# Differential attention: the four value projections move into the head loop, one ahead of every second head's value product

## The reference

```python
def diff_mixer(h, w_in, qk_norm_g, lam_vecs, subln_g, w_out, rel_table, lam_init):
    q, k, v = jnp.split(h @ w_in, [DIFF_QK, 2 * DIFF_QK], axis=-1)
    q = rms_norm(q.reshape(B, S, 8, 2, 64), qk_norm_g[0]) * (64 ** -0.5)
    k = rms_norm(k.reshape(B, S, 8, 2, 64), qk_norm_g[1])
    ...
    p1 = softmax(q1 @ k1.T + bias); p2 = softmax(q2 @ k2.T + bias)
    out = (p1 - lam * p2) @ v                       # per head, v is 256 x 128
    out = rms_norm(out, subln_g) * (1.0 - lam_init)
    return out.reshape(B, S, DIFF_V) @ w_out
```

## Time and profile before

| what | value |
|---|---|
| median of 3 runs | 1779.64 us (1777.1 to 1780.9) |
| the profiled execution | 1776.03 us, of which the span from first to last instruction is 1774.2 us |
| PE busy | 89% of the span |
| DVE, ACT, POOL busy | 52%, 41%, 8% |
| mean granted TensorE clock | 0.918 of full speed |
| the diff stage | about 887 to 1070 us of the span |

### The profile page before, as it was taken

One profiled execution on the slowest core, in us unless ns is written; L12 is line 12 of the kernel. 1 busy time (PEld: TensorE's weight loads), 2 busy tenths in 40 slices (PEclk: granted clock), 3 DMA queues, 4 the chain that ended last, 5 costly groups with the idle time before them and its releaser, 6 DMA issues.

```text
span 1774.2 us, 23807 instructions
## 1 busy us (share of the span) xinstructions
PE 1583.0 (89%) x10412; PEld 1437.9 (81%) x10412; DVE 916.0 (52%) x1006; ACT 728.0 (41%) x780; POOL 148.2 (8%) x147
## 2 busy tenths in 40 slices
PE   5999998588799999999998669999799987789997
PEld 4999997587689998999998459999777773679996
DVE  4666655667354445544545645444642246354443
ACT  4544543566244434443444434444432233244332
POOL 2000001055000000000023001000130000010000
PEclk9999997899899999999999779999886775789999
DMA  7788861412145554655584016555330011035551
GB/s 249 243 278 262 271 215 49 141 50 94 56 159 190 184 179 136 213 184 180 184 208 151 24 41 212 190 189 183 92 119 24 24 48 48 24 110 194 180 183 70
DMA packets 197777, 258.75 MB, mean 146 GB/s; under 512 B 4781, under 2 KB 178122, under 8 KB 197546
## 3 DMA queue, kind: packets, MB, share of 16 engines
q1 hardware_dynamic: 194672, 248.59, 42.9%
q0 software_dynamic: 2752, 8.57, 1.7%
q10 hardware_dynamic: 250, 0.08, 0.0%
HBM read 255.91 MB, written 1.31 MB: 145 GB/s over the span
## 4 chain that ended last, share of the span: by engine, by line
PE 75%; DVE 10%; POOL 5%; ACT 4%; issue 4%; DMA 1%; SPq 0%; DVEq 0%; POOLq 0%; ACTq 0%
PE bank L175 15%; PE bank L176 15%; PE bank L177 15%; PE acc L175 7%; PE acc L176 7%; PE acc L177 7%; DVE w_lo L155 3%; ACT w_hi L149 2%; PE bank L1752 2%; PE acc L1726 1%; POOL rstd L759 1%; POOL arena L734 1%; POOL arena L735 1%; PE acc L1794 1%; POOL rstd L310 1%
## 5 line engine op out<-in xcount | busy, mean ns | idle before, releaser
L155 DVE TENSOR_TENSOR w_lo<-w_raw,w_hi 128x2048 fp32r<-128x2048 f32 x236 | 548.7, 2326 | 498.3 <-ACT w_hi L149 498.3
L149 ACT ACTIVATE w_hi<-w_raw 128x2048 fp32r<-128x2048 f32 x236 | 448.8, 1908 | 385.6 <-PE bank L177 290.7
L175 PE MATMUL bank<-h_hi,w_hi 128*128 128x256 f32 (+1 forms) x1872 | 540.5, 289 | 8.2 <-DVE h_lo L266 5.1
L176 PE MATMUL bank<-h_lo,w_hi 128*128 128x256 f32 (+1 forms) x1872 | 538.9, 288 | 0.0
L177 PE MATMUL bank<-h_hi,w_lo 128*128 128x256 f32 (+1 forms) x1872 | 538.7, 288 | 0.0
L175 PEld LDWEIGHTS bank<-h_hi,w_hi 128*128 128x128 f32 x1872 | 363.6, 194 | 16.0 <-issue 12.8
L176 PEld LDWEIGHTS bank<-h_lo,w_hi 128*128 128x128 f32 x1872 | 363.4, 194 | 3.2
L177 PEld LDWEIGHTS bank<-h_hi,w_lo 128*128 128x128 f32 x1872 | 363.2, 194 | 1.9
L175 PE MATMUL acc<-w_hi,act_hi 128*128 128x512 f32 x416 | 164.0, 394 | 0.8 <-issue 0.8
L176 PE MATMUL acc<-w_lo,act_hi 128*128 128x512 f32 x416 | 163.4, 393 | 0.0
L177 PE MATMUL acc<-w_hi,act_lo 128*128 128x512 f32 x416 | 162.7, 391 | 0.0
(11 more groups left out here) (267 smaller groups left out, 1675.6 us busy)
## 6 DMA issues: line engine op xcount, KB each, us to landing
w_raw<-in_ffn_w_gu SPq DMA_DIRECT2D x88, 1024.0 KB, 5.1
w_raw<-in_ffn_w_down SPq DMA_DIRECT2D x44, 1024.0 KB, 4.9
w_raw<-in_w_ada SPq DMA_DIRECT2D x24, 1024.0 KB, 5.9
w_raw<-in_w_ffn_in SPq DMA_DIRECT2D x22, 1024.0 KB, 5.1
w_raw<-in_gla_w_in SPq DMA_DIRECT2D x12, 1024.0 KB, 5.4
w_raw<-in_diff_w_in SPq DMA_DIRECT2D x12, 1024.0 KB, 5.2
w_raw<-in_w_ffn_out SPq DMA_DIRECT2D x11, 1024.0 KB, 4.9
w_raw<-in_w_in SPq DMA_DIRECT2D x9, 1024.0 KB, 5.2
```

The source lines that it names most:

```text
L149: eng.activation(w_hi[:, slot, :], w_raw[:, slot, :], ACT.Copy).then_inc(sem("unit_hi"), 1)
L155: eng.tensor_tensor(w_lo[:, slot, :], w_raw[:, slot, :], w_hi[:, slot, :].bitcast(F32), ALU.subtract).then_inc(sem("unit_split"), 1)
L175: pe.matmul(out_, a[0], b[0], start=first, stop=False)
L176: pe.matmul(out_, a[0], b[1], start=False, stop=False)
```

## The change

Only the units 8 to 11 (v) move. PE and ACT do units 0 to 7 ahead of the attention, and ACT's squares follow unit 7's copy. In the head loop, heads 0, 2, 4 and 6 each get one unit, 8 + h/2: on PE between the scores of h+2 and the value product of h, into bank 3, with a wait for ACT's copy of it before the value product; on ACT after the copy of the transposed probabilities (`split_hi` of unit 11 + h/2 and the copy out of bank 3); on DVE the `split_lo` of unit 11 + h/2 between `combine(h)` and `output(h-1)`. The value products of even and odd heads now use the two halves of bank 2, and PE waits for one more output copy (`output(h-1)` in place of `output(h-2)`).

```diff
@@ -910,17 +910,16 @@
 
                 split_hi(eng, u + j + 3)
                 eng.wait_ge(sem("unit_used"), u + j + 1)
-                eng.activation(diff_qkv[:, j, :, :].rearrange("p t c -> p (t c)"), bank[j % 3][:, :], ACT.Copy)\
+                b = bank[j % 3] if j < 8 else bank[3]
+                eng.activation(diff_qkv[:, j, :, :].rearrange("p t c -> p (t c)"), b[:, :], ACT.Copy)\
                     .then_inc(sem("diff_copied"), 1)
 
-            for j in range(9):
+            for j in range(8):
                 unit(j)
             for t in range(2):
                 eng.wait_ge(sem("diff_copied"), 4 * t + 4)
                 c = slice(t * 4 * TT * UC, (t + 1) * 4 * TT * UC)
                 eng.activation(diff_sq[:, c], flat_qkv()[:, c], ACT.Square).then_inc(sem("diff_squared"), 1)
-            for j in range(9, N_DIFF_IN):
-                unit(j)
             eng.wait_ge(sem("diff_dots"), 2)
             eng.activation(diff_dot[:, :], diff_dot[:, :], ACT.Exp).then_inc(sem("diff_exp_dots"), 1)
             for hp in range(4):
@@ -945,6 +944,8 @@
                 if h >= 2:
                     eng.wait_ge(sem("diff_pv"), h - 1)
                 eng.activation(diff_pt[:, h % 2, :], bank[h % 2][:, :], ACT.Copy).then_inc(sem("diff_pt_ready"), 1)
+                if h % 2 == 0:
+                    unit(8 + h // 2)
             eng.wait_ge(sem("diff_o_copied"), DH)
             for t in range(TT):
                 eng.activation(diff_osq[:, t * D:(t + 1) * D], diff_o[:, t, :], ACT.Square)\
@@ -977,12 +978,10 @@
                 eng.tensor_reduce(ssq[:, t * n_group:(t + 1) * n_group],
                                   diff_sq[:, c].rearrange("p (g d) -> p g d", d=DDH), AX.X, ALU.add)\
                     .then_inc(sem("diff_sums"), 1)
-                split_lo(eng, u + 12 + t)
             eng.wait_ge(sem("mixer_rstd"), mixer_index(name, 1))
             g = flat_qkv()[:, 0:4 * TT * UC].rearrange("p (g d) -> p g d", d=DDH)
             eng.tensor_tensor(g, g, rstd[:, 0:n_group].unsqueeze(2).broadcast_to([P, n_group, DDH]), ALU.mult)\
                 .then_inc(sem("diff_scaled_q"), 1)
-            split_lo(eng, u + 14)
             eng.wait_ge(sem("diff_exp_dots"), 1)
             eng.scalar_tensor_tensor(diff_neg_lam[:, :], diff_dot[:, 1:2], LAM_INIT, diff_dot[:, 0:1], ALU.subtract,
                                      ALU.subtract).then_inc(sem("diff_lam"), 1)
@@ -1031,7 +1030,7 @@
             def output(h):
                 eng.wait_ge(sem("diff_pv"), h + 1)
                 eng.tensor_copy(diff_o[:, :, h * P:(h + 1) * P],
-                                bank[2 + h % 2][:, 0:TT * P].rearrange("p (t c) -> p t c", t=TT))\
+                                bank[2][:, (h % 2) * S:(h % 2 + 1) * S].rearrange("p (t c) -> p t c", t=TT))\
                     .then_inc(sem("diff_o_copied"), 1)
 
             logits(0)
@@ -1039,6 +1038,8 @@
                 if h + 1 < DH:
                     logits(h + 1)
                 combine(h)
+                if h % 2 == 0:
+                    split_lo(eng, u + 11 + h // 2)
                 if h >= 1:
                     output(h - 1)
             output(DH - 1)
@@ -1089,11 +1090,11 @@
             h0 = h_ready_before(name)
 
             def unit(j, h_wait=None):
-                b = bank[j % 3]
+                b = bank[j % 3] if j < 8 else bank[3]
                 natural_columns(pe, u + j, [b[:, 0:UC], b[:, UC:2 * UC]], S, h_wait)\
                     .then_inc(sem("unit_used"), 1)
 
-            for j in range(N_DIFF_IN):
+            for j in range(8):
                 if j >= 3:
                     pe.wait_ge(sem("diff_copied"), j - 2)
                 unit(j, None if j else h0)
@@ -1104,7 +1105,7 @@
                     pe.wait_ge(sem("diff_scaled_q"), 1)
                 if n == 4:
                     pe.wait_ge(sem("diff_scaled_k"), 1)
-                    pe.wait_ge(sem("diff_copied"), N_DIFF_IN)
+                    pe.wait_ge(sem("diff_copied"), 8)
                 b = acc_bank[n] if n < 4 else bank[n - 4]
                 for hh in range(2):
                     for t in range(TT):
@@ -1138,12 +1139,19 @@
                 last.then_inc(sem("diff_p_transposed"), 1)
                 if h + 2 < DH:
                     scores(h + 2)
+                if h % 2 == 0:
+                    if h >= 2:
+                        pe.wait_ge(sem("diff_copied"), 8 + h // 2)
+                    else:
+                        pe.wait_ge(sem("diff_k_ready"), 4)
+                    unit(8 + h // 2)
+                    pe.wait_ge(sem("diff_copied"), 9 + h // 2)
                 pe.wait_ge(sem("diff_pt_ready"), h + 1)
-                if h >= 2:
-                    pe.wait_ge(sem("diff_o_copied"), h - 1)
+                if h >= 1:
+                    pe.wait_ge(sem("diff_o_copied"), h)
                 for t in range(TT):
                     for k in range(TT):
-                        last = pe.matmul(bank[2 + h % 2][:, t * P:(t + 1) * P],
+                        last = pe.matmul(bank[2][:, (h % 2) * S + t * P:(h % 2) * S + (t + 1) * P],
                                          diff_pt[:, h % 2, k * S + t * P:k * S + (t + 1) * P],
                                          diff_qkv[:, 8 + h // 2, k, (h % 2) * P:(h % 2 + 1) * P],
                                          start=k == 0, stop=k == 1)
```

## The result

The median went from 1780.3 us (the kernel before, timed beside it) to 1816.1 us; the ratio is 1.0194 with an interval of 1.0162 to 1.0226. The forecast was 1811, range 1800 to 1819.

The account below looks back on a forecast made before the run. PE matmuls bound most of the kernel, but a chain off PE bounds the stretch ahead of the loop and a PE-DVE circle the loop. Loop +42.8 (41.4 plus clock 1.4), ahead -10.7: +32, forecast 1811 us, range 1800 to 1819.

Parts of the forecast that it names:

- VectorE's waits for `w_hi`: Sign in the head loop: DVE's largest wait would be on ACT's split, some 6 to 8 us each.
- Part 1: Ahead of the head loop: earlier squares and sums start POOL 9.3 us earlier, a removed split gives 1.4; 10.7 us gained.
- PE's idle time: Sign ahead of the loop: PE waits 22 us from 941, with scores of head 0 at about 970.3.
- The removal of VectorE's split: Ahead of the loop: without DVE's split queued before them, copies of k follow the transposes and scores start 1.4 us earlier.
- Part 2: Head loop: unit, ACT's split and DVE's split lie end to end, 10.5 us in heads 0, 2, 4, 9.9 in 6; together 41.4.
- the circle: Head loop's repeating dependency: transposes and scores on PE (3.17 or 1.77 us), then logits and combine on DVE (3.47 us).
- The clock, +1.4: Head loop: heads 1, 3, 5 run low (+3.2 us), heads 2 and 4 high behind a 5 us burst (-1.8).
- D: Rival, head loop: low clock in even heads too, units partly at half speed; +4 to +8 us, 1817; chance 11%.
- A: Rival, head loop: dense units keep the clock high through the gaps; -8.2 us, 1803, still slower; chance 12%.
- B: Rival, head loop: DVE runs ahead, logits(h+2) not behind the unit; even head 11.3 us, total +12.5, 1792; chance 3%.
- C: Rival, head loop: units hide in PE's idle time during DVE's work; loop 55.6 us, total +1.2, 1781; chance 4%.

Follow-up runs that it names:

- e7: Kernel before with only the change's banks: value products in two halves of bank 2, PE waiting for output(h-1); 1782.6 us, ratio 1.0006.
- e5: Kernel before, all units still ahead of the attention, with only ACT's squares moved behind unit 7 and VectorE's sums ahead of its splits; 1775.0 us, ratio 0.9962.
- e1: Changed kernel with VectorE's split of the next unit behind combine of the odd head instead of the even one; 1793.5 us, ratio 1.006.
- e3: Changed kernel with ScalarE, in the loop, copying the unit's product before splitting the next unit; 1818.5 us, ratio 1.0205.
- e10: Changed kernel with unread identity products in PE's gaps: 18 behind each unit, 16 behind the first scores, 6 behind each value product; 1802.2 us, ratio 1.0115.
- e2: Changed kernel with ScalarE copying before splitting and VectorE's split behind combine of the next even head, the last behind head 7; 1783.5 us, ratio 1.0012.
- e6: Kernel before with early squares and back-to-back sums, and VectorE's split of unit 14 moved behind the copies of k; 1772.6 us, ratio 0.995.
- e9: Kernel before with unread identity products on PE: 16 behind the scores of heads 0 and 1, 6 behind each value product; 1771.0 us, ratio 0.9934.
- e4b: Changed kernel with 18 unread identity products on PE behind each of the four units; 1807.6 us, ratio 1.0138.
- e4: Changed kernel with 64 unread identity products on PE behind each of the four units; 1838.4 us, ratio 1.0327.

## Why the prediction was right, point by point

The forecast was +32 us; the two lengths say +35.5 and the medians +35.9. One of the signs named in the forecast was mis-sized: VectorE's waits for `w_hi` are 11.0 us each in the mean and not 6 to 8, because they begin where VectorE ends its combine, and take in TensorE's transposes and scores as well. It has no part in the sum. The loop ended at 1067.3, not 1064.

- **Part 1, 10.7 us earlier.** 10.3 measured at the scores of head 0, counted from ACT's `w_hi` of unit 7; the 11.3 of the table has 1.0 more, which is the high clock of those scores (2.00 us, not 3.50), and luck, as e7 shows. The sums were done at 948.94 (944.46 + 4.48), 8.7 us behind ACT's `w_hi` of unit 7 and not 18.1 as before; the scores of head 0 started at 969.83 (forecast 970.3, and the earlier end of unit 7 alone moves them by 0.9). PE's idle time of 22.28 us was forecast as 22. The removal of VectorE's split: the copies of k began 1.1 us behind the start of their transposes, where 0.6 was forecast. The lock of the shared port, which the Trainium skill's page "SBUF — State Buffer" ("SBUF: two separate sides") describes, shows again in the changed kernel and in e5: a small operation of VectorE, queued in the place of the split, took from 962.19 to 965.77, the end of GpSimd's scaling (960.02 + 5.73 = 965.75). Timeline of VectorE; the same operation took 0.15 us in the kernel before:

```profile
962.19 3.58 DVE L986 SCALAR_TENSOR_TENSOR arena<-arena 128x1 f32<-128x1 f32 x1
```

- **Part 2, the unit and both splits on the circle.** Right in kind (chain, waits, e1 against e3) and in size: with the clock held up (e10) head 2 takes 15.74 us. Measured in the changed kernel: 16.96, 17.31, 17.29 and 14.55 for heads 0, 2, 4 and 6.
- **The clock, +1.4.** This is the term that was mis-sized: about +5.4 in place of +1.4 (46.8 - 41.4). Odd heads were right (6.68). Heads 2 and 4 were forecast at the high clock, 15.74, and took 1.6 more each; head 6 took 14.55 and not 13.4. The step that failed is the sentence that heads 2 and 4 come behind a 5 us burst and so run high, as head 1 did: they ran high for the transposes only (0.66 and 0.69), then low for the scores and the beginning of the unit. Each unit ran partly at the low clock: 6.46, 6.66, 6.61 and 7.23 us from its start to ACT's `w_hi` at granted clocks of 0.93, 0.90, 0.91 and 0.79, against a pitch of 5.76. For heads 0 to 5 e10 shows that nothing but the clock was missing. Why the clock fell after 0.66 us of transposes in one place and not in another is left open.
- **Rivals.** D (low clock everywhere, 1817) came half true, and 1816.1 lies nearer to it than to 1811: its units partly at half speed are there, and the transposes and scores of heads 2 and 4 took 2.67 and 2.70 us, between the 1.77 of the forecast and the 3.17 of D. A (clock kept up by the units, 1803) did not occur; e10 brought it about with its fillings, 1802.2. The granted clock over the loop was 0.77 in the changed kernel, with idle times of 1.3 to 5.0 us but for the last, and 0.92 in e2, with 0.7 to 1.6 in its middle (periods of 14.56 us with 1.77 for the odd head's transposes and scores). The page "TensorE: Matmul & The Clock Gate" of the Trainium skill ("Why this matters for your kernels") names both halves, dense work and no idle gaps, and these two loops agree with it. B and C did not occur, for the reason given, and e1 and e2 brought them about: 1793.5 (worked out 1792) and 1783.5 (worked out 1781). In e1 only head 2 has B's length (11.20, worked out 11.3); heads 0 and 4 took 14.7 and 14.8, at a granted clock of 0.74. By the page "Perfetto Trace Analysis" of the Trainium skill ("Optimization Strategy") interleaving may help; here its best form is level with the kernel before, since the four units still lengthen the loop by 17 us, and only 11.7 are gained ahead.
- **No load is late.** Right: SP's loads waited for splits, and no `w_hi` in the loop waited for a DMA.

## What to carry to other kernels

An engine's idle time inside a loop of dependent steps is not free room: what is put there brings its helpers' operations with it, and each of them lands in some in-order queue, ahead of the step that the loop is waiting for. Before moving work, write down for every engine what stands behind the moved operation's wait; here one `split_lo` ahead of the logits made the difference of 18 us in the loop. And take the two halves of such a change apart: the half that started the long chain earlier was a gain by itself (e5), and the move of the units was its whole loss.

## What the runs showed of the hardware

- The granted clock in a loop of short bursts can't be told from the last burst alone. The same head loop ran with periods of 5.3 to 6.7 us in the kernel before and in e7, with 6.66 to 6.69 in all six in e6, and with 5.28 in e9, where 1.5 us of products that nobody reads were added per head. The loop of e6 was 4.1 us longer than in the kernel before, nearly half of the 9.1 that e6 gained ahead. But e7, whose start had not moved, was 2.3 longer too, so how much of it comes from the moved start is not shown.
- Dummy products pay when they fit the gap and cover each gap: 4 us behind the unit alone (e4b) gave 2.3 us, all gaps (e10) 11.3. An f32 product of 128 columns is two matmuls of 0.11 us at the high clock, so 64 of them took 14.3 us and overran gaps of 2.5 and 4.8 (e4).
- Transposes alone raised the clock. In the changed kernel TensorE had been idle for 22.3 us; the first 16 transposes took 3.65 us at a granted clock of 0.50, the next 16 took 2.46, and the scores of heads 0 and 1 behind them 2.00 at 1.00.
- The mixed stage comes in two lengths, some 6 us apart, with the same code. Why an execution falls into the one or the other was not tried.
